# Gate spreading in a hybrid encoder step: one of three gate products per four tokens moved from ScalarE to GpSimd

## The reference, cut to what matters

```python
eid = jnp.take_along_axis(cand_id, top_pos, axis=-1)          # i * 128 + j, 128 picks for each token
gate = jax.nn.softmax(top_s, axis=-1).astype(xn.dtype)
...
hid = jnp.einsum('td,ted->te', xb, u_tab[eb])
return jnp.einsum('te,ted->td', jax.nn.gelu(hid, approximate=False) * gb, v_tab[eb])
```

## Time and profile before

| | before |
|---|---|
| median of 3 runs | 2727.44 us (2725.97 to 2730.17) |
| the profiled execution's own time | 2724.83 us |
| its span | 2722.8 us |
| PE (TensorE, matmul) | 2509.6 us busy, 92% |
| PEld (TensorE, weight load) | 2446.0 us busy, 90% |
| DVE (VectorE) | 1550.2 us, 57% |
| ACT (ScalarE) | 968.2 us, 36% |
| POOL (GpSimd) | 651.8 us, 24% |
| granted TensorE clock, mean | 0.952 |
| L1718, products of one-hot matrices | x1152, 146.8 us busy |
| L1738, gate products on ACT | x432, 394 ns each |
| L1792 / L1795 on DVE | 1083 / 600 ns each (mean), x144 each |
| L1758, bank copies on ACT | x144, 585 ns each |
| L1705, low parts on POOL | x18, 2579 ns each |

### The profile page before, as it was taken

One profiled execution on the slowest core, in us unless ns is written; L12 is line 12 of the kernel. 1 busy time (PEld: TensorE's weight loads), 2 busy tenths in 40 slices (PEclk: granted clock), 3 DMA queues, 4 the chain that ended last, 5 costly groups with the idle time before them and its releaser, 6 DMA issues. The chain is left out here.

```text
span 2722.8 us, 48234 instructions
## 1 busy us (share of the span) xinstructions
PE 2509.6 (92%) x18910; PEld 2446.0 (90%) x18910; DVE 1550.2 (57%) x2800; ACT 968.2 (36%) x1818; POOL 651.8 (24%) x313
## 2 busy tenths in 40 slices
PE   7977888887899899899979999999999998999997
PEld 6976778787799899888879999999999998999997
DVE  4334554633678776677745454454554543677774
ACT  3335334422332232688853322322322221222222
POOL 2433343423254545111122211211211210000000
PEclk9997899868999899999989999999999999999999
DMA  5331000003233233366664323323323322454551
GB/s 182 114 106 41 24 24 1 13 1 128 65 98 96 90 102 102 115 181 191 193 209 150 112 94 110 112 94 110 112 94 110 112 94 78 153 175 158 191 174 40
DMA packets 162452, 296.11 MB, mean 109 GB/s; under 512 B 11873, under 2 KB 99233, under 8 KB 158121
## 3 DMA queue, kind: packets, MB, share of 16 engines
q1 hardware_dynamic: 162344, 294.61, 32.9%
HBM read 230.26 MB, written 64.31 MB: 108 GB/s over the span
## 5 line engine op out<-in xcount | busy, mean ns | idle before, releaser
L115 PE MATMUL banks<-w_high,v_high 128*128 128x288 f32 x2048 | 605.4, 296 | 12.0 <-issue 11.6
L117 PE MATMUL banks<-w_high,v_low 128*128 128x288 f32 x2048 | 605.6, 296 | 0.0
L116 PE MATMUL banks<-w_low,v_high 128*128 128x288 f32 x2048 | 604.3, 295 | 0.0
L115 PE MATMUL banks<-res_hi,u_high 128*128 128x288 f32 x1440 | 428.6, 298 | 11.7 <-ACTq L2004 10.9
L117 PE MATMUL banks<-res_hi,u_low 128*128 128x288 f32 x1440 | 425.7, 296 | 0.0
L116 PE MATMUL banks<-res_lo,u_high 128*128 128x288 f32 x1440 | 425.4, 295 | 0.0
L115 PEld LDWEIGHTS banks<-w_high,v_high 128*128 128x128 f32 x2048 | 385.2, 188 | 15.5 <-issue 11.8
L117 PEld LDWEIGHTS banks<-w_high,v_low 128*128 128x128 f32 x2048 | 385.3, 188 | 0.0
L116 PEld LDWEIGHTS banks<-w_low,v_high 128*128 128x128 f32 x2048 | 385.2, 188 | 0.0
L1998 DVE TENSOR_TENSOR res_x<-banks,res_x 128x288 f32<-128x288 f32 x512 | 225.4, 455 | 280.7 <-PE banks L117 280.7
L1618 POOL TENSOR_TENSOR u_low<-u_raw,u_high 128x1024 fp32r<-128x1024 f32 x72 | 183.6, 2551 | 707.1 <-ACT u_high L1614 707.1
(11 more groups left out here) (327 smaller groups left out, 4473.5 us busy)
## 6 DMA issues: line engine op xcount, KB each, us to landing
v_raw<-arg_v SPq DMA_DIRECT2D x128, 512.0 KB, 3.9
scratch_gates<-gate_stage SPq DMA_DIRECT2D x18, 2048.0 KB, 9.3
u_raw<-arg_u SPq DMA_DIRECT2D x36, 1024.0 KB, 5.8
gates_in<-scratch_gates SPq DMA_DIRECT2D x32, 1152.0 KB, 7.2
q_raw<-arg_u SPq DMA_DIRECT2D x38, 512.0 KB, 3.6
scratch_hidden<-gelu_ahead SPq DMA_DIRECT2D x56, 288.0 KB, 2.4
gelu_out<-scratch_hidden SPq DMA_DIRECT2D x56, 288.0 KB, 2.9
in_raw<-arg_w_in SPq DMA_DIRECT2D x25, 512.0 KB, 4.0
```

Of the source, the lines that this page charges most:

```text
L115: pe.matmul(out, ah, bh, start=first, stop=False)
L116: pe.matmul(out, ah, bl, start=False, stop=False)
L117: return pe.matmul(out, al, bh, start=False, stop=last)
```

## The change

The gate product of the third second key (t = 2) leaves ScalarE's `gate`, which now does two, and goes to GpSimd as a multiplication of two tensors (the one-hot matrix, in place, and its gate spread over 128 columns), once a group. GpSimd waits for `onehots` there, as ScalarE does, and counts a new semaphore `thirds`, for which TensorE waits at each group and VectorE at each step's start. GpSimd's subtractions for the low parts now stand behind the third products of group 3 (s = 0) and of group 6 (s = 1).

```diff
+        thirds = core.sem("third_seconds_gated")
...
+        LOWS = {3: 0, 6: 1}
...
             @block.gpsimd
             def _(pool):
                 pool.sem_inc(u_low, 2)
+                pool.sem_inc(thirds, 1)
                 with pool.Fori(0, steps) as it:
-                    for s in range(2):
-                        pool.wait_ge(u_high, it * 2 + s + 1)
-                        pool.tensor_tensor(ul[:, s], u.raw[:, s, 0], uh[:, s].bitcast(F32), ALU.subtract).then_inc(u_low, 1)
+                    for g in range(PER):
+                        pool.wait_ge(onehots, it * PER + g + 1)
+                        o = pair[:, g % SLOTS, FOUR + ACT_T - 1, :]
+                        pool.tensor_tensor(o, o, curg[:, g, ACT_T - 1:ACT_T].broadcast_to([P, N_KEYS]),
+                                           ALU.mult).then_inc(thirds, 1)
+                        if g in LOWS:
+                            s = LOWS[g]
+                            pool.wait_ge(u_high, it * 2 + s + 1)
+                            pool.tensor_tensor(ul[:, s], u.raw[:, s, 0], uh[:, s].bitcast(F32),
+                                               ALU.subtract).then_inc(u_low, 1)
...
                         pe.wait_ge(lasts, it * PER + g + 2)
                         pe.wait_ge(gated, it * PER + g + 2)
+                        pe.wait_ge(thirds, it * PER + g + 2)
...
                 def gate(it, g):
                     act.wait_ge(onehots, it * PER + g + 1)
-                    for t in range(ACT_T):
+                    for t in range(ACT_T - 1):
...
                     dve.wait_ge(lasts, it * PER + 1)
+                    dve.wait_ge(thirds, it * PER + 1)
```

## The result

The changed kernel takes 2753.72 us (median of 4 runs, 2745.2 to 2754.6) beside 2727.28 us before (median of 4, 2725.97 to 2730.17): ratio 1.0088, 95% interval 1.0067 to 1.011. It is slower by 26 us. A second set of runs gave 2748.94 us (5 runs) beside 2727.42, ratio 1.0081 (1.0067 to 1.0095), so the change costs 22 to 26 us. The forecast was 2764, range 2743 to 2776: side and range held, but the size was forecast as 37 us and the measured one is some 30 to 40% less.

A forecast was written before the change was run, and what follows sets the result against it. TensorE, busy 92% of the span, was taken as the bound; a + b = +2.55 us a step gave +23 over nine steps, the clock +14, together +37, forecast 2764 us, range 2743 to 2776.

The forecast's parts named there:

- Term a, the earlier start: Ahead of group 0, one ScalarE product slot goes, so TensorE starts each step 0.29 us earlier.
- The subtraction ends at 7.02 however early ScalarE is: On GpSimd, the first subtraction waits for VectorE's group 6 comparison and still ends 7.02 us behind group 0's start.
- Term b, the first half later: Group 4 waits for its third product behind GpSimd's subtraction; the first half starts at 10.44, not 7.60: +2.84 us a step.
- I take VectorE as first: At 7.02 VectorE's group 7 comparison starts before GpSimd's third product and holds to 8.10; group 4 starts at 8.50.
- side case (7.56): GpSimd gets in ahead of the group 7 comparison: group 4 starts at 7.56, about +18 us, 2745, without the clock.
- Term c, the clock: The 4.4 us gap between groups 3 and 4 lowers TensorE's granted clock each step: +1.6 us, nine times +14.
- From there to the step's end TensorE is full: From the first half's start at 7.60 to the step's end, TensorE has no idle time.
- The second subtraction hidden: Group 7's third product waits for the second subtraction, but TensorE is in the half until 13.6, which hides it.
- No lock: GpSimd's subtraction ends at 6.25, group 4 starts at 6.8, no clock fall: +0.85 us a step, +8, 2735; chance 0.05.
- Queue without the clock: GpSimd's queue delays group 4 but the clock seldom falls: +23 us, 2750, or about +18, 2745; chance 0.23.
- Dear product: A third product takes 0.81 us on GpSimd and VectorE bounds the stage: +46 us, 2773; chance 0.10.
- Relief carries: Group 4's third product is done before TensorE asks, so group 4 follows ScalarE: -0.8 us a step, 2720; chance 0.04.

The follow-up runs named there:

- cover_18: Changed kernel with 18 TensorE products of constant data put behind group 3 to fill the gap; 2753.0 us, 1.0105 against the kernel before.
- cover_gap: Changed kernel with 16 TensorE products of constant data put behind group 3 to fill the gap; 2757.4 us, 1.0118 against the kernel before.
- lows_4_7: Changed kernel with GpSimd's subtractions behind the third products of groups 4 and 7 in place of 3 and 6; 2739.1 us, 1.0043 against the kernel before.
- lows_5_6: Changed kernel with GpSimd's subtractions behind the third products of groups 5 and 6 in place of 3 and 6; 2724.6 us, 0.9997 against the kernel before.
- relief_only: Kernel before with the third gate product of each group left out, so one of four tokens is not gated; 2719.0 us, 0.9976 against the kernel before.
- lows_5_8: Changed kernel with GpSimd's subtractions behind the third products of groups 5 and 8 in place of 3 and 6; 2718.8 us, 0.9971 against the kernel before.
- cover_wide: Changed kernel with 8 constant-data TensorE products of 512 columns put behind group 3 to fill the gap; 2750.0 us, 1.0087 against the kernel before.
- halves_6_9: Changed kernel, next step's first gate products ahead of ScalarE's last gelu, s = 0 halves and subtractions behind groups 6 and 9; 2721.1 us, 0.9972 against before.
- after: The changed kernel against the kernel before, first set of runs; 2753.7 us, 1.0088.
- after_again: The changed kernel run again with no edit, against the kernel before; 2748.9 us, 1.0081.

## Why the prediction was right, and by how much it was off

The order of things was right: the queue on GpSimd, then the lock, then the clock. In the total some luck helped. Without the clock the prediction had 2745 to 2750, and 2749 to 2754 was measured, so the time alone speaks for that rival more than for the forecast of 2764. The step of 34.15 us is even the 34.1 that the prediction named as the sign against the clock, had it come at a full clock; it came at 0.95. The other terms were too dear by about what the clock costs. Only the rows of the clock and cover_18 tell the two apart. In numbers, for a step (predicted; measured):

- **Term a, the earlier start:** -0.29; -0.34. Right.
- **The subtraction ends at 7.02 however early ScalarE is:** 7.01. Right, and with it the reason: the comparison for group 6 keeps GpSimd out until it ends. ScalarE's side came as worked out too (high part at 2.74, products of group 4 done at 4.37; 2.73 and 4.36 predicted).
- **Term b, the first half later:** +2.84; +2.22. The step that failed is "I take VectorE as first". The third product of group 4 went in ahead of the comparison for group 7, and group 4 started at 7.62, not 8.50. The prediction had this as a side case (7.56) and chose the other. Two smaller errors hide part of the 0.88. Group 5 does not follow at once: its third product stands behind the comparison for group 7 (1.25 us long), and at a full clock, in cover_18, groups 4 and 5 take 2.34 where I had 1.94. And the first half began at 7.52 in the kernel before, not at 7.60. In cover_18 it begins at 9.74, 2.22 later.
- **Term c, the clock:** +1.6; +1.19. It falls in each of the eight later steps, and TensorE works 1.5 us longer when it does, as the pairs of steps show (1.5 in cover_gap and lows_4_7), but in the changed kernel 1.2 of it reaches the step. Where the other 0.3 goes is argued and not shown: about 0.2 us of the half clock lies ahead of group 4, where TensorE is idle, and part of the loss falls where group 5 waits anyway (2.34 in cover_18 for two groups, which at the pace of groups 6 to 8, 2.84 for three, would take about 1.97).
- **Missing from the sum:** -0.52. Groups 6 to 12 follow each other closer when ScalarE has less to do (0.18 and 0.34). I had written "From there to the step's end TensorE is full", and put this part at nothing. Its records did touch, but groups of the same instructions took longer, so it was not full. In groups 0 to 3 the same is worth 0.27, and is inside term b.

Together -0.34 + 2.22 + 1.19 - 0.52 = +2.55, beside +2.56 measured; predicted +4.15. The prediction took nine such steps. Measured, the first step is 1.3 us longer (it has no second fall in the profiled execution), seven are 2.56 longer, and the last, counted to the end of its last half, 2.9: the 22 us of the stage.

- **The second subtraction hidden:** it was in the changed kernel, where nothing waits at groups 7 and 8. With the first half back at 7.56 (lows_5_6) it costs 0.6 a step.
- **Rivals.** No lock: refuted by the 7.01 and by the 1.08 to 1.28 of the comparison. Queue without the clock: refuted, a fall in each later step of both profiled executions, and a step 1.19 shorter where the falls were taken away. Dear product: 0.44 us, not 0.81. Relief carries: its size was right by luck (-0.8 a step predicted, -0.77 in relief_only), but by other groups than I said; and its condition, a product of group 4 that stands ahead of the subtraction, is what lows_5_8 gives.

## What to carry to other kernels

When work is moved to an idle engine, look at what already stands in its queue and where the moved piece lands among it: here two numbers, {3, 6} or {5, 8}, made the difference between 0.9% slower and 0.3% faster, with the same instructions on every engine. An engine that shows no idle time in its records can still be paced by its feeder: compare the pitch of the same instructions in two stretches before counting it as full. And a wait on TensorE can cost more than its length: 1.2 us of the step here, once the clock falls behind it.

## What the runs showed of the hardware beyond the expected

- The granted clock fell behind gaps shorter than I had thought from the earlier trace rows. In the eight later steps, by the longest gap: 3.79 us, 8 of 8; 2.08, 5 of 8 (lows_4_7); 1.97, 7 of 8 (cover_wide); 1.70, 2 of 8 (cover_gap); 1.45, none (cover_18). The kernel before has 1.67 in each step and no fall. The longest gap does not decide it. In halves_6_9 no gap is longer than 1.04, and one step of eight has a fall, behind three gaps of 0.64, 0.88 and 1.04 within 6 us. And in the first step of the changed kernel a gap of 3.15 brought no fall in one execution (`after`), one of 3.33 did in the other (after_again). No run here shows which of two like steps gets the fall. One fall, to 0.50 for 3.4 us, costs 1.5 us of TensorE time where TensorE is busy through it.
- GpSimd's 128x128 product and VectorE's comparison with two inputs from SBUF hold each other up both ways: the comparison goes from 1.08 to 1.28 us, the product from 0.39 to as much as 1.26, and a 1024-column subtraction from 2.35 to 3.2. The Trainium skill ("SBUF — State Buffer", section "SBUF: two separate sides") has the pair of ports held for a full instruction by whoever starts first. The trace agrees on the order, but by the records the holds are shorter than the instruction. VectorE's small instruction, 0.34 us by itself, ends 0.08 us behind the subtraction, so by this reckoning it was let in about 0.26 before the subtraction's record ends. Of a product's 0.44 us, 0.2 reach the comparison.
- Sixteen or eighteen more products in TensorE's loop brought a single wait of 16 us for "issue" at the entry of the next stage's loop; with eight (of 512 columns) it was absent. That it comes from the place of the code is a guess that no run here tests.
